# A hybrid SSD and attention layer on one core: one shared weight ring, a late norm factor, and the decode state's update moved to TensorE

## What is computed

```python
h = rmsnorm(x)
z, xbc, dt, q, kv, ... = split(h @ w_in)
xbc = silu(causal_dwconv(xbc))                 # x: 2048 channels, B and C: 4 groups x 128
# Mamba-2 scan: h_t = exp(dt_t a) h_{t-1} + dt_t x_t B_t^T ;  y_t = h_t C_t + d x_t
#   prompt: exact in chunks of 128 positions; sample: one step from a stored state (8, 32 heads, 64, 128)
o_ssd = rmsnorm(y * silu(z)) @ w_ssd_o         # gated, then merged
...                                            # sparse attention, memory attention, merge
x = x + mixed @ w_out
u = causal_dwconv(rmsnorm(x) @ w_up, width 3)  # 2 x 2816 channels
x = x + (silu(u1) * u2) @ w_down
```

## Time and profile before

| | us |
|---|---|
| median of 3 runs (1820.5 to 1822.06) | 1821.2 |
| the profiled execution, device time | 1823.51 |
| its span in the trace | 1821.7 |
| PE busy | 1668.1 (92%) |
| DVE / POOL / ACT busy | 940.2 / 697.7 / 692.8 |
| mean granted clock of TensorE, share of full | 0.957 |
| scan, merge_ssd, project_nsa, compress_rows begin at about | 283, 427, 584, 738 |
| the up-projection's first matmul | 1425.5 |

### The profile page before, as it was taken

How to read it: one execution, slowest core, us unless ns; L and a number is a source line. 1 busy time by engine, 2 the same in 40 slices (tenths; PEclk the granted TensorE clock), 3 DMA queues, 4 the chain that set the end, 5 groups by cost and what they waited for, 6 DMA issues and landing times. The chain is left out here.

```text
span 1821.7 us, 33695 instructions
## 1 busy us (share of the span) xinstructions
PE 1668.1 (92%) x13060; PEld 1515.0 (83%) x13060; DVE 940.2 (52%) x1533; ACT 692.8 (38%) x1402; POOL 697.7 (38%) x362
## 2 busy tenths in 40 slices
PE   6999996886997999779998998989989799999999
PEld 5999994555997999536666898988889799999999
DVE  4477766996511353246774255442133588777200
ACT  4333336884511331135554333333322333333211
POOL 2344446993343333124443341012243244444343
PEclk9999998998999999879999999999999899999999
DMA  4222225543222432214002324535424122222233
GB/s 146 72 92 92 92 70 195 196 150 116 80 87 70 148 104 99 97 45 165 1 0 71 139 92 142 184 119 219 148 70 151 58 93 91 89 88 90 83 87 121
DMA packets 60397, 193.65 MB, mean 106 GB/s; under 512 B 6964, under 2 KB 19764, under 8 KB 56756
## 3 DMA queue, kind: packets, MB, share of 16 engines
q1 hardware_dynamic: 58996, 190.30, 30.9%
q10 hardware_dynamic: 1312, 2.14, 0.4%
HBM read 174.47 MB, written 22.14 MB: 108 GB/s over the span
## 5 line engine op out<-in xcount | busy, mean ns | idle before, releaser
L257 POOL TENSOR_TENSOR mm_ring<-mm_raw,mm_ring 128x1024 fp32r<-128x1024 f32 x110 | 270.6, 2462 | 555.6 <-ACT mm_ring L234 427.5
L234 ACT CAST mm_ring<-mm_raw 128x1024 fp32r<-128x1024 f32 x120 | 125.7, 1049 | 357.8 <-PE up_pp L267 228.9
L267 PE MATMUL up_pp<-h,mm_ring 128*128 128x260 f32 x2016 | 244.0, 284 | 3.0 <-POOL mm_ring L257 3.0
L267 PEld LDWEIGHTS up_pp<-h,mm_ring 128*128 128x128 f32 x2016 | 243.8, 189 | 3.2 <-ACT up_conv_s L2951 3.2
L267 PE MATMUL ssd_pp<-h,ssd_ring 128*128 128x260 f32 x1920 | 233.2, 284 | 3.0 <-POOL ssd_ring L257 3.0
L267 PEld LDWEIGHTS ssd_pp<-h,ssd_ring 128*128 128x128 f32 x1920 | 232.6, 190 | 3.2 <-ACT gates_raw L518 3.2
L267 PE MATMUL up_pp<-act_t,mm_ring 128*128 128x260 f32 x1344 | 163.6, 284 | 6.7 <-POOL mm_ring L257 6.7
L267 PEld LDWEIGHTS up_pp<-act_t,mm_ring 128*128 128x128 f32 x1344 | 163.1, 190 | 7.1 <-issue 7.1
L257 POOL TENSOR_TENSOR ssd_ring<-mixed,ssd_ring 128x1024 fp32r<-128x1024 f32 x42 | 102.3, 2438 | 168.3 <-ACT ssd_ring L234 153.0
L267 PE MATMUL nq_pp<-h,nq_ring 128*128 128x260 f32 x960 | 122.4, 289 | 10.5 <-POOL nq_ring L257 10.5
L267 PEld LDWEIGHTS nq_pp<-h,nq_ring 128*128 128x128 f32 x960 | 119.4, 192 | 11.4 <-issue 10.7
(11 more groups left out here) (423 smaller groups left out, 2991.4 us busy)
## 6 DMA issues: line engine op xcount, KB each, us to landing
mm_raw<-in_w_up SPq DMA_DIRECT2D x44, 512.0 KB, 3.7
mixed<-in_w_ssd SPq DMA_DIRECT2D x42, 512.0 KB, 3.5
mem_ring<-in_mem_kv SPq DMA_DIRECT2D x16, 1024.0 KB, 6.4
ms_raw<-in_w_ssd_merge SPq DMA_DIRECT2D x24, 512.0 KB, 3.6
mm_raw<-in_w_mkv_qm SPq DMA_DIRECT2D x24, 512.0 KB, 3.8
nq_raw<-in_w_qk SPq DMA_DIRECT2D x20, 512.0 KB, 3.6
sc_seg<-cum_rows SPq DMA_DIRECT2D x16, 512.0 KB, 5.0
mixed<-in_ssd_state SPq DMA_DIRECT2D x16, 512.0 KB, 3.9
```

The costliest lines, as they stand in the source:

```text
L234: act.copy(self.ring[:, b % 2, 0], self.raw[:, b % 2]).then_inc(self.high, 1)
L257: pool.tensor_tensor(self.ring[:, u, 1], self.raw[:, u], self.ring[:, u, 0].bitcast(F32), ALU.subtract).then_inc(self.low, 1)
L267: last = pe.matmul(out(n), self.ring[:, b % 2, wn, k], x[:, xn, chunk + k, part], start=start and k == 0 and wn + xn == 0, stop=stop and k ...
```

## The change

Three changes go together.

**One weight ring.** A ring of 24 KB a partition at a fixed place (`shared`, at `ring_at`) serves all streams from `w_ssd_merge` on. The last stage before a stream's own loads its first two pieces, casts them and subtracts: `scan` does it for `w_ssd_merge`, `merge_ssd` for `w_qk` (`following`). The scan's decay rows `sc_seg` lie over the split half of the ring, so ACT's casts there wait until POOL has read them (`mixed_up`). The stores of `project_ssd` and of `project_nsa` are no longer waited for in their own stage but at the end of the next one (`conv_stored`, `rows_stored`), and the convolution stores wait for the convolution only.

**The sample's state.** It now lies with the 128 state entries on partitions and 1024 channels of one sample along the free axis. Diagonals, spread, `outers`, the eight products and the sum are gone. Once, PE turns x and B of the samples into rows (`rows_of_sample`) and spreads all decays. For each sample ACT keeps, of the eight rows of B, only that sample's (`own_rows`; `gate` and `diagonals` have left POOL). In each step PE makes the outer product as two matmuls of 8 rows (`outer_product`) and reads the state with eight matmuls of one column (`read_state`), DVE multiplies by the decay (`decay`) and adds the product (`step`). The gate is on DVE and goes in place in PSUM.

**The norm's factor.** The up-projection's input is x times the gain, without the factor; it is split while `w_out` is still being multiplied (`take_high`, `split_chunk`). The factor is multiplied in when DVE brings a tile out of PSUM (`evacuate`), and ACT makes the first tap (`first_tap`). The two matmuls for the total stand behind `multiply_pair`.

```diff
+        shared = Ring(top.over("mm_raw", [P, 2, KC, P], F32, ring_at + 4 * chunk),
+                     top.over("mm_ring", [P, 2, 2, KC, P], F32R, ring_at))
...
@@ scan, SP, behind its loop @@
+            for b in range(2):
+                following.load_piece(sp, 0, b)
             sp.wait_ge(state_done, STEPS)
...
+            sp.wait_ge(conv_stored, 32)
...
@@ scan, POOL, behind its loop @@
+            pool.wait_ge(mixed_up, STEPS)
+            for b in range(2):
+                following.write_low_of(pool, 0, b)
...
@@ scan, PE @@
-                pe.matmul(pbs[:].rearrange("p a b n -> p (a b n)"), c["ones"][:],
-                          diag[:, v % 2].rearrange("p a b n -> p (a b n)"), start=True, stop=True).then_inc(on_rows, 1)
+            def outer_product(v):
+                q, half = v // 2, v % 2
+                pe.wait_ge(owned, q + 1)
...
+                    pe.wait_ge(stepped, v)
+                for m in range(2):
+                    rows = slice(32 * (2 * half + m), 32 * (2 * half + m) + DEC)
+                    mm = pe.matmul(xb[:, m, :], own[rows, q % 2, :], xr[rows, :], start=True, stop=True)
+                mm.then_inc(outer, 1)
+            def read_state(v):
+                q, half = v // 2, v % 2
+                pe.wait_ge(stepped, v + 1)
+                for n in range(HC):
+                    ch = half * HC + n
+                    mm = pe.matmul(ys[:, ch, q:q + 1], ring[:, v % TT, n * P:(n + 1) * P],
+                                   xbct[:, DI + GROUPS + ch // PER, SEQ + q:SEQ + q + 1], start=True, stop=True)
+                mm.then_inc(read_out, 1)
...
                 if v:
-                    pe.wait_ge(gained, v)
+                    pe.wait_ge(gated, v)
                 pe.wait_ge(mixed_up, v + 1)
...
@@ scan, ACT, behind its loop @@
+            for b in range(2):
+                act.wait_ge(mixed_up, STEPS - AHEAD + 2 * b + 1)
+                following.write_high(act, 0, b)
...
@@ scan, DVE @@
+                dve.tensor_tensor(st, st, dec[:, heads, q].unsqueeze(2).broadcast_to([P, SSD_HEADS // 2, HEAD_P]),
+                                  ALU.mult).then_inc(decayed, 1)
...
+                dve.wait_ge(outer, v + 1)
+                dve.tensor_tensor(st, st, xb[:], ALU.add).then_inc(stepped, 1)
...
             for v in range(STEPS):
+                if v:
+                    gate(v - 1)
+                decay(v)
+                if v and v + 1 < STEPS:
+                    weigh(v + 1)
+                step(v)
                 take_in(v)
...
@@ merge_ssd, SP, POOL and, behind its loop, ACT @@
+                sp.wait_ge(w.low, w.total - 1 + b)
+                following.load_piece(sp, 0, b)
+                following.write_low_of(pool, 0, b)
+            following.write_first_after(act, w)
...
@@ project_nsa, SP @@
-            sp.wait_ge(stored, 48)
...
@@ finish_layer, PE @@
+            w_up.multiply_pair(pe, lambda b, n: pp[:, 0, b, n, 0:HALF], h, HALF_PARTS, low)
             pe.wait_ge(gathered, KC - 1)
             for n, part in enumerate(HALF_PARTS):
                 mm = pe.matmul(total[:, n, 0:HALF], c["ones"][:], sq_sum[:, part], start=True, stop=True)
             mm.then_inc(summed, 1)
-            pe.wait_ge(evacuated, 1)
-            w_up.multiply_pair(pe, lambda b, n: pp[:, 0, b, n, 0:HALF], h, HALF_PARTS, low)
...
@@ finish_layer, DVE @@
+                w_up.finished(dve, i, u)
+                for m in range(2):
+                    ins = dve.tensor_tensor(halves(pad[:, u, m, FCONV - 1:]), pp[:, u, m, :, 0:HALF], halves(r[:]), ALU.mult)
...
-                    o(dve.tensor_scalar(acc[:, u, m, PROMPT], pad[:, u, m, 0:SEQ], tap(0), tap(FCONV), ALU.mult,
-                                        ALU.add))
```

More of the change, by code:

```diff
@@ L122, in retire_semaphores, with hold @@
     @staticmethod
+    def hold(semaphores):
+        for sem in semaphores:
+            Stage.taken.remove(sem)
+    @staticmethod
     def retire_semaphores(nc):
@@ L618, in _ @@
                 o.leave(rounds)
+    return stored
 LOG1P_TERMS = 7
@@ L955, in _ @@
                 if v + 1 < STEPS:
-                    rows_of_sample(v + 1)
+                    outer_product(v + 1)
+            for v in range(STEPS - 2, STEPS):
+                read_state(v)
             turn_y(STEPS - 1)
@@ L1254, in project_nsa @@
         t2 = s.sb("nq_t2", [P, COLS])
+        assert nc.sbuf_base <= end, (nc.sbuf_base, end)
         pp = s.ps("nq_pp", [P, 2, 2, 512])
@@ L1277, in _ @@
             pages.load_table(sp)
-            for b in range(2):
-                w.load_piece(sp, 0, b)
             for t in range(2, w.tiles):
@@ L2946, in turn @@
                         w_down.write_first_after(act, w_up)
-                    w_up.finished(act, i, u)
-                    act.wait_ge(convolved, t + 1)
-                    for m in range(2):
-                        act.copy(halves(pad[:, u, m, FCONV - 1:]), pp[:, u, m, :, 0:HALF])
-                    act.copy(conv_s[:, bass.ds(t, 1), :, :].rearrange("p a m (s k) -> p (a m) s k", k=FCONV)[
-                        :, :, :, FCONV - 1], pp[:, u, :, 1, HALF - DEC:HALF]).then_inc(evacuated, 1)
+                    if not (first and u == 0):
+                        silu(t - 1, 1 - u)
+                    first_tap(t, u)
                     if not (first and u == 0):
```

327 lines of the change are left out of this document (160 added, 167 removed).

## The result

The changed kernel takes 1841.3 us (median of 4 runs, 1839.54 to 1845.61) against 1821.08 for the kernel before: 1.0111 times as long, 95% interval 1.0096 to 1.0127. The forecast was 1811.5 with a range of 1797 to 1829. The sign is wrong, and the time lies outside the range. The profiled execution took 1840.58 us, its span is 1838.8, 17.1 more than the span before.

What follows compares the result with a forecast made beforehand. TensorE was taken as busy most of the span, with the scan paced by DVE and POOL. Terms -2.1 -1.5 +12 -3.0 -5.0 -4.8 -4.0 -1.3 gave -9.7, from profiled 1823.5 to 1813.8, less 2.3: 1811.5, range 1797 to 1829.

Steps and rivals of the forecast that it cites:

- Scan start: Start of the scan: ACT no longer waits for two convolution stores, only the meeting of the engines stays; -2.1 us.
- scan end: Scan to merge_ssd: first two weight pieces are loaded, cast and subtracted in the scan, 13.5 us instead of 16.5; -3.0 us.
- project_nsa: merge_ssd to project_nsa: loads and first cast go under the last pieces, 5.5 us gap in place of 10.5; -5.0 us.
- start of the up-projection: Up-projection start: x times gain split under the output projection, PE goes on earlier, 1.3 given back for clock; -4.0 us.
- down-projection: Start of the down-projection: the last tile's chain loses two first taps and 0.4 us before them; -1.3 us.
- What moved onto VectorE in the up-projection's loop: Up-projection loop: DVE gets two products and loses two taps per tile, 200 us of 244, so hidden.
- compress_rows: project_nsa to compress_rows: stores go on under the next stage, 5.4 less, 0.6 back for queued weights; -4.8 us.
- the read-out's price: Scan step: eight one-column matmuls taken at 1.1 us, within a 7.9 us step against 7.99; -1.5 us over 15 steps.
- the clock: Scan: light PE work and waiting bring 3.4 us stretches at 0.50, one in every other step; +12 us, between 0 and 25.
- The prediction's own sign: Profile after: scan PEclk over 0.95, or a step over 9.5 us, would show the forecast's middle term wrong.
- the rival on the slow side: Scan: lower clock holds it, a little over one fall per step costs 30 instead of 12, 1829.5 us; 15%.
- The other rivals: Scan: clock stays up, 1799.5 us, 17%; or the outer product's two matmuls don't run side by side, 1825 us, 8%.

Runs made afterwards that it cites:

- the best parts: Changed kernel with the scan as before, third up-projection piece cast ahead of Ln, and project_nsa's stores behind the compression's loads: 1796.38 us, 0.9872 of the kernel before.

## Why the prediction was wrong

**Right: the ends of stages.** Scan start -2.1 forecast, -3.0 measured; scan end -3.0, -4.05; project_nsa -5.0, -4.5; start of the up-projection -4.0, -5.1 (the clock did fall behind the gap, but it had done so before as well, so the 1.3 us given back for it weren't needed in the difference); down-projection -1.3, -1.1. Each was a chain of few instructions with rows for all of them. What moved onto VectorE in the up-projection's loop is hidden, as forecast: DVE is busy 210.60 of 243.79 us there, forecast 200.

**Half right: compress_rows.** The gap shrank by 5.7, forecast 5.4. But 0.6 was set down for the loads behind the stores, between nothing and 2, and 2.95 came back, outside those bounds: the load that counts is a small one that lands 6.5 us after its issue, and DVE's copies are queued behind the wait for it. What was late next was looked for at the weights, not at the first small load. The kernel of the best parts shows it: with the loads first the wait is 2.9.

**Wrong, first: the read-out's price.** The text said "I take 1.1", below the row that it called nearest (1.3) and far from its upper bound, the sixteen records of line 953 with a load each, 2.00 us. It takes 1.84 at the full clock. Sixteen records of one column cost nearly what sixteen of 64 columns cost. With it the step at the full clock is about 8.6 in place of 7.9; 0.74 us in each of the 14 read-outs of the stretch are 10 us.

**Wrong, second and more: the clock.** The direction was right, and so was the doubt that waits alone bring it down. The size was not: "I take one in every other step, +12, the middle". The trace has one fall in nearly each step from the sixth on, 3.4 us each, and 33 us at 0.50 in the first five: 69 us in all, which by the estimate above cost some 29 in place of 12, more than the upper bound that the text worked out (25). It took 3.4 us for a fall where its own row, has 6.80 at 0.50; in the first five steps most are as long as that or longer. The middle between two bounds had no row behind it: falls in every other step do occur in these runs, with the read-out ahead of the outer product, but no row of the kernel before could tell which of the two it would be. The prediction's own sign has it so: its middle term is wrong if the step is over 9.5 us, and it is 10.29.

The forecast of the rival on the slow side had the mechanism, "a little over one fall in each step", 2.0 us each, and the point from which it decides, 1.45 us a step; the loss is 1.9. With the read-out's 10 us added it gives 1829.5 + 10 = 1839.5, near the 1841.3 measured; the other misses, among them 2.4 us at the start, 2 in compress_rows and as much the other way at the ends of stages, nearly cancel. Both misses were priced alone and not together; the range held one of them at a time.

The other rivals are excluded: the pair does run side by side (1.13 us), and the clock does not stay up.

On the Trainium skill's page "TensorE: Matmul & The Clock Gate", section "HAM oscillation — how this bites in real kernels", the fall follows idling between bursts. In these runs a wait of up to 1.0 us in 14 steps went without any fall, which does not speak against the page, whose example has longer waits. But a scan in which PE was busy 99% had a fall in nearly every step, and the same instructions in another order had few: here idling alone did not decide.

## What to carry to other kernels

Work moved to TensorE to relieve other engines is priced twice: by its time, and by what it does to the clock of what follows; in this scan, steps with matmuls of few rows and few columns side by side took longer than the work that they replaced. Where light matmuls can't be avoided, try other places for them, between full-width ones first, and look at the granted clock step by step: moving one call between two others was worth some 25 us here, and putting it off at the changes of group cost more than that. And where a wait for stores is moved away, issue the next stage's first small loads ahead of those stores.

## What the runs showed of the hardware that was not expected

- A PE that is busy 139.74 of 141.70 us had a mean granted clock of 0.86; with the same instructions in two other orders it was 1.00 (busy 122.11 of 137.40 us) and 0.95 (125.55 of 127.70).
- The same kernel, with the read-out between the two products and 8 rows, took from 1810.43 to 1832.94 us in eight runs, at a mean clock over the execution from 0.960 down to 0.947.
- A matmul of one column with a 128 x 128 load takes 0.115 us a record at the full clock (1.84 for sixteen); sixteen of 64 columns take 1.9.
- In the up-projection's loop DVE's instructions of line 3033 took 2.39 us on the mean (1.37 for the same product before), without any effect on PE, whose 2016 products there took 243.79 and 243.78 us.
